# Router logits of a fused transformer kernel taken from the raw residual: scaled router weights, a shift row, and both tiles' expert choices in one stretch

## The reference, cut to what matters

```python
        x_new = x + ga * merge_heads(o_diff, o_mla, subln_w[l], lam_init, w_out[l])
        ...
        hf = modulate(rmsnorm(x, ffn_norm_w[l]), sf, scf)      # rmsnorm(x)*w * (1 + scf) + sf
        x = x + gf * moe(hf.reshape(B * n, D), router_w[l], router_b[l], w1[l], b1[l], w2[l], b2[l])
...
def moe(h, router_w, router_b, w1, b1, w2, b2):
    logits = (h @ router_w + router_b).astype(jnp.float32)
    top_v, top_i = lax.top_k(logits, TOP_K)                    # 4 of 32 experts
    gates = jax.nn.softmax(top_v, axis=-1).astype(h.dtype)
    ...                                                        # each expert on its tokens
```

## Time and profile before

| | before |
|---|---|
| median of 3 runs | 1494.36 us |
| the profiled execution's own time | 1493.45 us |
| its span, first to last instruction | 1491.7 us |
| PE busy | 1377.5 us (92%) |
| DVE busy | 503.7 us (34%) |
| ACT busy | 312.8 us (21%) |
| POOL busy | 45.2 us (3%) |
| mean granted TensorE clock | 0.981 |
| HBM traffic | 335 GB/s over the span, 428 to 429 GB/s in most slices of the expert loop |

### The profile page before, as it was taken

One profiled execution on the slowest core, in us unless ns is written; L12 is line 12 of the kernel. 1 busy time (PEld: TensorE's weight loads), 2 busy tenths in 40 slices (PEclk: granted clock), 3 DMA queues, 4 the chain that ended last, 5 costly groups with the idle time before them and its releaser, 6 DMA issues.

```text
span 1491.7 us, 17451 instructions
## 1 busy us (share of the span) xinstructions
PE 1377.5 (92%) x6828; PEld 741.6 (50%) x6828; DVE 503.7 (34%) x898; ACT 312.8 (21%) x454; POOL 45.2 (3%) x70
## 2 busy tenths in 40 slices
PE   4998999989999889899998999999988899999998
PEld 2884455433434324333343343343333387889987
DVE  2846435113113111131131121111311347755566
ACT  3515233101101001011011010010110354544451
POOL 2000002100000000000000000000000101000000
PEclk9999999999999999999999999999999999999999
DMA  9319906999999999999999999999999853565540
GB/s 389 119 38 369 426 12 222 406 428 429 429 429 429 429 427 429 429 428 427 428 428 428 429 429 427 428 429 429 429 429 429 347 209 111 171 195 180 189 142 29
DMA packets 61898, 500.01 MB, mean 335 GB/s; under 512 B 5192, under 2 KB 21864, under 8 KB 34144
## 3 DMA queue, kind: packets, MB, share of 16 engines
q1 hardware_dynamic: 59616, 492.85, 80.2%
q0 software_dynamic: 2032, 6.05, 1.4%
q10 hardware_dynamic: 208, 0.54, 0.1%
HBM read 498.37 MB, written 1.05 MB: 335 GB/s over the span
## 4 chain that ended last, share of the span: by engine, by line
PE 65%; DMA 22%; DVE 7%; issue 3%; ACT 1%; SPq 1%; DVEq 0%; ACTq 0%; PEldq 0%
PE bank L1560 28%; DMA ring<-in_w 20%; PE bank L637 17%; PE bank L675 15%; PE bank L695 2%; DMA ring<-in_w_ada 2%; DVE dk L750 1%; DVE mrows L754 1%; DVE dk L744 1%; PE bank L683 1%; PE bank L657 1%; PE bank L648 1%; SPq L592 0%; PE bank L1747 0%; DVE psum_sum L1282 0%
## 5 line engine op out<-in xcount | busy, mean ns | idle before, releaser
L637 PE MATMUL bank<-ring,xn 128*64 128x512 f32 x2048 | 467.9, 611 | 64.7 <-DMA ring<-in_w 64.7
L637 PEld LDWEIGHTS bank<-ring,xn 128*64 128x64 f32 x2048 | 162.0, 140 | 360.4 <-issue 360.2
L675 PE MATMUL bank<-ring,dq 128*64 128x512 f32 x1024 | 226.8, 595 | 0.0
L709 ACT ACTIVATE sq<-mrows 128x512 f32<-128x512 f32 x32 | 19.6, 630 | 773.8 <-DVE mrows L739 773.8
L739 DVE TENSOR_SCALAR mrows<-bank 128x512 f32<-128x512 f32 x32 | 20.6, 686 | 476.6 <-PE bank L637 476.6
L675 PEld LDWEIGHTS bank<-ring,dq 128*64 128x64 f32 x1024 | 70.6, 137 | 136.5 <-issue 136.5
L763 DVE TENSOR_TENSOR dk<-bank,bc 128x512 f32<-128x512 f32 x32 | 22.1, 692 | 236.2 <-PE bank L675 236.2
L494 DVE TENSOR_TENSOR w_lo<-ring,w_hi 128x2048 fp32r<-128x2048 f32 x34 | 77.7, 2291 | 33.2 <-ACT w_hi L489 33.1
L1560 PE MATMUL bank<-x_hi,w_hi 128*128 128x256 f32 x256 | 72.5, 283 | 0.8 <-DVE h_lo L1439 0.8
L1560 PE MATMUL bank<-x_hi,w_lo 128*128 128x256 f32 x256 | 72.5, 283 | 0.0
L1560 PE MATMUL bank<-h_lo,w_hi 128*128 128x256 f32 x256 | 72.5, 283 | 0.0
(11 more groups left out here) (413 smaller groups left out, 1512.1 us busy)
## 6 DMA issues: line engine op xcount, KB each, us to landing
ring<-in_w SPq DMA_DIRECT2D x192, 2048.0 KB, 17.1
ring<-in_w_ff SPq DMA_DIRECT2D x32, 1024.0 KB, 5.4
ring<-in_w_ada SPq DMA_DIRECT2D x24, 1024.0 KB, 16.5
ring<-in_w_out SPq DMA_DIRECT2D x8, 1024.0 KB, 10.6
ring<-in_w_in SPq DMA_DIRECT2D x8, 992.0 KB, 25.7
ring<-in_w_in SPq DMA_DIRECT2D x8, 640.0 KB, 11.4
ring<-in_w_ple_gate SPq DMA_DIRECT2D x4, 1024.0 KB, 4.8
xc<-in_ctx SPq DMA_DIRECT2D x1, 1024.0 KB, 4.9
```

The source lines that it names most:

```text
L637: m = pe.matmul(banks[bank_no][mine(i), :], gathered[:, k, mine(i)], rows_of(at + i, 2)[:, k % 2, q * 512:(q + 1) * 512], start=k == 0, st ...
L675: m = pe.matmul(banks[OUT_BANKS[c]][mine(i), :], actT[:, k, mine(i)], rows_of(8 + 2 * j + i, 4)[:, r, c * 512:(c + 1) * 512], start=k == 0 ...
L709: act.activation(sg[:, cols], gs[:, cols], ACT.Sigmoid, scale=ALPHA).then_inc(moe("sigmoid", which), 1)
```

## The change

It moves the router's product in front of the normalisation.

- **New in the attention stage.** After unit 5's value product TensorE turns the rows `bc[0:1, 1]` (shift sf) and `bc[0:1, 2]` (scale s) into columns: 16 transposes of 1x128 into a new tile `columns`. ACT copies them out. POOL, which now loads the router weights after unit 7's scores, multiplies these by both columns (`rw_shift`, `rw_scaled`).
- **In the output products.** After the first quarter of tile 1's products, TensorE transposes tile 0's residual (8 transposes, tiles `x1T0_0`, `x1T0_1`).
- **Behind the output products.** TensorE makes the shift row (9 matmuls of 32 columns), tile 0's logits (8), turns tile 1's residual, and makes tile 1's logits in two halves around the ranking of tile 0. The transposes of `hf` and the separate bias matmul of each tile are gone.
- **DVE.** Tile 0's `choose` stands behind tile 1's mean square; both choices lie in one stretch. `hf` of tile 1 is made afterwards, in two halves by four fused instructions of 256 columns (`second_rows`), from `x1_scaled` that two plain products of 512 columns prepare. The gate weights are computed behind the first `select`.
- **gather** of pair 0 waits for the halves of tile 1's `hf` (`hf_done` 3 and 4).

```diff
+    if _what == "value" and _u == 5:
+        FRONT_TILES.append("columns")
...
+ROUTER_TILES = ["x1T0_0", "x1T0_1", "router_shift", "logits0", "x1T1_0", "x1T1_1", "logits1", "rank"]
...
+                if y_read is None and k % 4 == 0:
+                    pe.wait_ge(sem("hf_done"), 3 + k // 4)
...
+            wait_read(pool, "columns")
+            pool.wait_ge(sem("router_in"), 32)
+            for n, dst in enumerate((rw_shift, rw_scaled)):
+                step(pool.tensor_tensor(dst, rw, columns[:, n, :].unsqueeze(2).broadcast_to([P, KD, E]), ALU.mult),
+                     "router_scaled")
...
             for n in range(2):
                 act.wait_ge(sem("x1_done"), 3 + n)
                 step(act.activation(xn[:, 0, 0:512], xc[:, 3, n * 512:n * 512 + 512], ACT.Square,
                                     accum_out=stat[:, 8 + n:9 + n]), "ss2_done")
+                if n == 0:
+                    b = take(act, "router_shift")
+                    step(act.activation(router_shift[:], b[:, 0:E], ACT.Copy), tile="router_shift")
+                residual_turned(1, n)
...
+                if t:
+                    step(V.tensor_tensor(x1_scaled[:, 0:512], xc[:, 3, 0:512], bc[:, 2, 0:512], ALU.mult))
+                dve.wait_ge(sem("ss2_done"), 2 * t + 1)
+                if t:
+                    step(V.tensor_tensor(stat[:, 1:2], stat[:, 8:9], stat[:, 9:10], ALU.add))
+                step(V.tensor_scalar(stat[:, 2 + t:3 + t], stat[:, t:t + 1], 1.0 / D, EPS, ALU.mult, ALU.add), "ms_done")
+                if t:
+                    wait_read(dve, "router_shift")
+                    choose(0)
+                    step(V.tensor_tensor(x1_scaled[:, 512:D], xc[:, 3, 512:D], bc[:, 2, 512:D], ALU.mult))
+                dve.wait_ge(sem("root_done"), 4 + t)
...
+            second_rows(0)
+            b = take(dve, "rank")
...
+            select(dve, 0, 0, MAIN)
+            second_rows(1)
...
+                if what == "value" and u == 5:
+                    wait_read(pe, "bc5")
+                    b = claim(pe, "columns")
+                    for n in range(2):
+                        for k in range(KD):
+                            m = pe.transpose(b[:, n * KD + k:n * KD + k + 1], bc[0:1, 1 + n, k * P:(k + 1) * P], ident[0:1, 0:1])
...
+                    elif j == 1:
+                        pe.wait_ge(sem("x1_done"), 2)
+                        for h in range(2):
+                            turn_residual(0, h)
...
+            pe.wait_ge(sem("router_scaled"), 2)
+            b = claim(pe, "router_shift")
+            for k in range(KD):
+                mm(b[:, 0:E], ones[:], rw_shift[:, k, :], k == 0, False)
+            mm(b[:, 0:E], ones[0:1, :], rb[:], False, True).then_inc(full("router_shift"), 1)
+            router_product(claim(pe, "logits0"), 0, range(KD)).then_inc(full("logits0"), 1)
+            pe.wait_ge(sem("x1_done"), 3)
+            turn_residual(1, 0)
+            pe.wait_ge(full("wo1_1"), use("wo1_1") + 1)
+            pe.sem_inc(freed, 1)
+            pe.wait_ge(sem("x1_done"), 4)
+            turn_residual(1, 1)
+            b1 = claim(pe, "logits1")
+            router_product(b1, 1, range(0, 4))
             pe.wait_ge(sem("below_done"), 1)
             b = claim(pe, "rank")
             pe.wait_ge(sem("chosen_done"), 1)
             mm(b[:, 0:E], below, chosen[:, 0, :], True, True)
             mm(b[:, E:2 * E], ones[:], chosen[:, 0, :], True, False)
-            wait_read(pe, "hfT1_3")
-            keep_running(bank("hfT1_3"), 1)
+            router_product(b1, 1, range(4, KD)).then_inc(full("logits1"), 1)
+            keep_running(3)
             pe.wait_ge(sem("chosen_done"), 2)
```

More of the change, by code:

```diff
@@ L967, in _ @@
                     step(act.activation(probT[:, u % 2, :], b[:], ACT.Copy), tile=f"pT{u}")
+                elif what == "value" and u == 5:
+                    b = take(act, "columns")
+                    step(act.activation(columns[:], b[:, 0:2 * KD].rearrange("p (n k) -> p n k", n=2), ACT.Copy), tile="columns")
                 elif what == "value" and u == 9:
@@ L980, in _, with residual_turned @@
             step(act.activation(stat[:, 4:5], stat[:, 2:3], ACT.Sqrt), "root_done")
[L981 to L987, removed]
+            def residual_turned(t, j):
+                b = take(act, f"x1T{t}_{j}")
+                step(act.activation(x1T[:, 4 * j:4 * j + 4, t * P:(t + 1) * P], b[:].rearrange("p (k t) -> p k t", k=4),
+                                    ACT.Copy), tile=f"x1T{t}_{j}")
+            for j in range(2):
+                residual_turned(0, j)
             for n in range(2):
@@ new lines, in _ @@
+                dve.wait_ge(sem("root_done"), 4 + t)
+                step(V.reciprocal(stat[:, 6 + t:7 + t], stat[:, 4 + t:5 + t]))
+                if t == 0:
+                    for n in range(2):
+                        cols = slice(n * 512, n * 512 + 512)
+                        step(V.scalar_tensor_tensor(out=sq[:, 0:512], in0=xc[:, 2, cols], scalar=stat[:, 6:7],
+                                                    in1=bc[:, 2, cols], op0=ALU.mult, op1=ALU.mult))
+                        step(V.tensor_tensor(by_twos(hf[:, 0, cols], True), by_twos(sq[:, 0:512]), by_twos(bc[:, 1, cols]),
+                                             ALU.add), "hf_done")
+                    dve.wait_ge(sem("iota_done"), 1)
+                    step(V.tensor_copy(iota_s, iota_i))
+                    step(V.tensor_copy(iota_e[:], iota_i[:, 0:E]))
+                    step(V.memset(gates[:], 0.0))
+                    step(V.memset(slots[:], -1.0))
+                else:
+                    choose(1)
@@ new lines, in second_rows @@
+            def second_rows(half):
+                for n in (2 * half, 2 * half + 1):
+                    cols = slice(n * 256, n * 256 + 256)
+                    step(V.scalar_tensor_tensor(out=hf[:, 1, cols].rearrange("p (r s) -> p r s", r=2),
+                                                in0=x1_scaled[:, cols].rearrange("p (s r) -> p r s", r=2), scalar=stat[:, 7:8],
+                                                in1=bc[:, 1, cols].rearrange("p (s r) -> p r s", r=2),
+                                                op0=ALU.mult, op1=ALU.add), "hf_done" if n % 2 else None)
@@ L1780, in _, with turn_residual, router_product @@
                 m.then_inc(full(f"mixT{j}"), 1)
+            def turn_residual(t, j):
+                b = claim(pe, f"x1T{t}_{j}")
+                for kk in range(4):
+                    k = 4 * j + kk
+                    m = pe.transpose(b[:, kk * P:(kk + 1) * P], xc[:, 2 + t, k * P:(k + 1) * P], ident[:])
+                m.then_inc(full(f"x1T{t}_{j}"), 1)
+            def router_product(b, t, ks):
+                for k in ks:
+                    if k % 4 == 0:
+                        wait_read(pe, f"x1T{t}_{k // 4}")
+                    m = mm(b[:, 0:E], x1T[:, k, t * P:(t + 1) * P], rw_scaled[:, k, :], k == 0, k == KD - 1)
+                return m
             bw = {(t, n): claim(pe, f"wo{t}_{n}") for t in range(NT) for n in range(2)}
```

92 lines of the change are left out of this document (27 added, 65 removed).

## The result

| | before | after |
|---|---|---|
| median (lowest to highest, runs) | 1494.3 us (1493.01 to 1496.34, 14) | 1498.94 us (1495.86 to 1500.29, 14) |
| ratio after / before | | 1.0026, 95% interval 1.0019 to 1.0033 |
| the profiled execution's own time, span | 1493.45, 1491.7 us | 1499.49, 1497.8 us |
| mean granted TensorE clock | 0.981 | 0.977 |

The change makes the kernel slower: by 3.9 us going by the ratio (1494.3 x 0.0026, interval 2.8 to 4.9), by 4.6 going by the medians. The prediction said 1498.7 with 1494.8 to 1501.3.

What follows compares the result with a forecast made beforehand. The weight stream bounds the kernel and starts a fixed time after the first expert matmul, so delays ahead of it count fully. Terms 1.9 + 1.0 + 1.4 = +4.3 us on 1494.36 gave 1498.7, range 1494.8 to 1501.3.

Steps and rivals of the forecast that it cites:

- What sets the time: Expert loop: transfers set the pace; the weight stream resumes a fixed 8.1 us after the first expert matmul.
- A: Attention stage, TensorE: sixteen 1x128 transposes into columns, not hidden, 0.12 us each, +1.9 us; bounds 0.5 to 3.2.
- B: Inside tile 1's output products: tile 0's eight transposes delay their end, +1.0 us.
- E: Moment the output products end; as a forecast term: transfers (router weights, second block's tables) cost 0, overlap up to 0.7.
- C: From E to pair 0's gather: ACT's second square waits, clock halves; gather at E + 17.4 against 16.0, +1.4 us.
- D: Gather of pair 0: about the same share at half clock as before, 0.
- the attention stage's clock: Attention stage: where the clock falls may move, by about 1 us either way.
- The clock did not stay up: Rival behind the output products: clock stays at 1.00 up to the gather, +0.7, 1495.1 us; chance 0.17.
- Narrow instructions did not cost what their columns cost: Rival for TensorE's narrow instructions: 0.03 us each, shorter chain and columns, -3.8, 1490.6 us; chance 0.02.
- The gather at half clock: Worse case, pair 0's gather: all at half clock, 6.9 us, +2.4, total 1501.1; worse cases together 0.05.

Runs made afterwards that it cites:

- e3: Changed kernel with the shift row's nine matmuls moved into the attention stage, ahead of unit 11's value product; 1496.2 us, 1.0009 of the kernel before.
- e4: Changed kernel with unread 256-column matmuls put back, five behind tile 0's logits and four ahead of its ranking; 1498.33 us, 1.0027 of the kernel before.
- e5: Changed kernel with the edits of e2 and e3 together; 1490.88 us, 0.9971 of the kernel before.
- e2: Changed kernel with both of tile 1's squares on ACT ahead of the copies it waits for; 1497.39 us, 1.0017 of the kernel before.
- e1: Changed kernel with the sixteen one-column transposes issued twice; 1499.37 us, 1.0033 of the kernel before.
- e6: e3 with tile 0's logits and choice inside tile 1's output products and five unread wide matmuls behind them; 1491.04 us, 0.9968 of the kernel before.
- e7: e6 without the unread wide matmuls (the two `keep_running`); 1492.58 us, 0.9978 of the kernel before.
- e8: Kernel before plus only the sixteen one-column transposes and ACT's copy of them, used by nothing; 1496.23 us, 1.0007 of the kernel before.

## Why the prediction was right

- **What sets the time.** That the stream's start follows the first expert matmul held: from that matmul to the loop's end it is 933.9 us before and 933.6 after, 932.9 in e3 and 932.75 in e4. The stream's next issue is at 265.94, 7.3 us after the matmul (forecast 8.1, counted to the window in which the share had risen; before, it was 261.15 - 253.89, also 7.3, and so it is in every experiment).
- **A, forecast +1.9, measured +1.1 in the row, +1.3 on the path.** The step was mis-sized. I priced the transposes like instructions of 32 columns, 0.12 us each; their row gives 1.14 / 16 = 0.07. With the slower starts of their neighbours they cost 1.3: from 171.03 to 174.17 the same instructions take 3.14 us, before from 170.79 to 172.64 they took 1.85. Both lie inside the bounds of 0.5 to 3.2. The Trainium skill, TensorE: Matmul & The Clock Gate, section "LDWEIGHTS (loading the stationary operand)", says that a load costs its columns / 1.2 ns whatever its rows; that makes an estimate of 107 ns for these 128 columns. The trace does not agree: with weights of one row it has 0.07 us for load and product together. It does not bear out the 25 ns that the prediction cites either.
- **B, forecast +1.0, measured 1.04 in the row** (eight transposes at 224.74), and 0.9 at E: the output products last 28.35 us with them (207.57 to 235.92), before 27.47.
- **C, forecast +1.4, measured +2.0.** The chain went as told, half a microsecond late at nearly every point: the mean square at E + 7.3 (forecast 6.7), `choose(0)` at E + 7.7 (7.2), `choose(1)` at E + 12.6 (11.9), the gather at E + 18.0 (17.4). These 0.6 come of the clock, which fell at about E + 3.3, not E + 4, so that tile 0's 16 logits instructions took 2.75 us instead of 1.9. ACT waited 4.9 us between the squares (forecast some 4), TensorE 1.25 ahead of tile 0's ranking (forecast 2). That ACT's order decides is shown by e5 against e3; in e2 the wait is gone as well, but its gain is less clear of the clock. The size of C is less sure than its place: e1, with the same program behind E, had +0.6 (16.6) where the changed kernel had +2.0.
- **D, forecast 0, measured +0.3.** The half clock lasted until about 256, the first 2.1 us of the gather. At full clock it takes 3.81 (e1, e2, e5, e6), before 4.53, after 4.82.
- **E, forecast 0, measured 0.** The tables now run where the queues were idle, up to the stream's start, and the loop takes no longer for it.
- **What no step had.** E moved by 2.5 us, of which A and B account for 2.2. Most of the other 0.3 stood already ahead of the columns (170.53 against 170.29), the rest is the attention stage's clock, a term named as up to 1 us either way; over the kernels here it was larger. The sum forecast for the first expert matmul was +4.3, the profile has +4.8, the measured ratio +3.9 (2.8 to 4.9). A's error (-0.6 to -0.8) and those of C and D (+0.9) cancel, so that the total is nearer than its terms is luck in part.
- **The rivals.** The clock did not stay up, as it fell with TensorE busy 3.00 of 3.00 us. The rule of the Trainium skill, TensorE: Matmul & The Clock Gate, section "What's actually happening", that activity releases the throttle, does not agree with this window if activity is read as busy time. Narrow instructions did not cost what their columns cost: 16 of 32 columns in a row took 1.87 at full clock, 0.12 each. (That rival let the chain of C start 3.1 us earlier; with the residual complete at E + 1.7 and the chain at E + 4.1 its own rows allow only 2.4.) The gather at half clock (+2.4) did not come in full either: it took 4.82, where 32 instructions at half clock would be 6.9.

## What to carry to other kernels

Before an in-order engine's program gets a new instruction that waits, look at what stands behind it: here two copies that nobody needed yet held up a square that everybody needed. Work taken off the critical stretch should go where the engine is idle: there 2.1 us of shift row cost 0.2. The columns and the eight transposes, put where TensorE had no idle time, cost 1.3 and 0.9 us, about what their rows say (1.14 and 1.04). When the bound is a stream that starts with a certain instruction, count everything up to that instruction and nothing behind it.

## What the runs showed of the hardware

- **The clock fell though TensorE was busy all the time.** In the changed kernel it is busy 3.00 of 3.00 us with 32-column instructions at 1.00, and the clock is 0.51 in the next three. In e6, with five unread matmuls of 256 columns in the stretch, it stayed at 1.00; in e7, without them and with idle time in their place, it was 0.50 in 244 to 248, at a cost of some 1.5 us. That is one profile of each; the medians differ the same way, but their intervals overlap.
- **The dips in the clock differ between kernels at places that no edit touches**, and move E and the end by up to two microseconds. With the same front, E stands at 235.92 in the changed kernel and at 234.00 in e4; the difference arises in the attention stage, where the changed kernel was at half clock from 194.6 to 198.2 and e4 was not. Behind the loop it cost the changed kernel 1.7 us. e1 and the changed kernel have one program behind E, and their stretches are 16.6 and 18.0 long. A part of the spread of E (e3 and e6, some 2 us) was there at 163 us already. Two single profiles therefore can be compared in their totals only to some 2 us, and stretches have to be compared from an anchor such as E. Why a dip comes in one kernel and not in another is open.
- **A one-row transpose to one column costs 0.07 us** at full clock (16 in 1.14 in the changed kernel and in e8, 32 in 2.13 in e1), about half of an instruction with 128 x 128 weights (0.12 to 0.13 us).
